# A two-layer encoder trunk on one core: GpSimd's copies and adding transfers form four input blocks of the MLP's up product

## The chip, the cores and the metric

The kernel runs on one core of a Trainium2 chip. Its engines are TensorE (PE, matrix products into the PSUM banks), VectorE (DVE), ScalarE (ACT), GpSimd (POOL) and SyncE (SP); the last two mostly start transfers here, which run on the core's 16 DMA engines. Each engine works through its own queue in order, and the queues wait for each other by semaphores alone. The metric is the device time of one execution in microseconds, as the median of runs; less is better.

## The reference

```python
def sqrelu_mlp(h, w_up, w_down):
    a = jax.nn.relu(h @ w_up)
    return (a * a) @ w_down

def reference(x, norm_mix, conv_w_in, conv_w, conv_w_out, attn_w_qkv, attn_rpb,
              attn_w_o, norm_mlp, mlp_w_up, mlp_w_down, norm_final):
    for i in range(DEPTH):
        h = rmsnorm(x, norm_mix[i])
        ...
            x = x + short_conv_mixer(h, conv_w_in[j], conv_w[j], conv_w_out[j])
        ...
            x = x + neighborhood_attention_2d(h, attn_w_qkv[j], attn_rpb[j], attn_w_o[j])
        h = rmsnorm(x, norm_mlp[i])
        x = x + sqrelu_mlp(h, mlp_w_up[i], mlp_w_down[i])
    return rmsnorm(x, norm_final)
```

DEPTH is 2, the sequence has 512 tokens of 1024 features, the MLP is 4096 wide, and everything is float32.

## The kernel before

**Every float32 product is three products.** An operand is split into a rounding (w_h, a_h, hx), made by ScalarE, and a rest (w_l, a_l, and the second half of hx), made by VectorE as operand minus rounding; TensorE multiplies rounding by rounding, rounding by rest and rest by rounding (L588 to L590). The weights come in 282 units w of 128x1024. For each unit ScalarE does hi(w) (L908), which waits for the unit's data and for TensorE to have finished unit w-4; VectorE does lo(w) (L1178), which waits for hi(w); TensorE waits for the lo of the unit that it starts. w_h and w_l have four slots each.

**Big products are done in seven instead of eight block products.** The matrices of the MLP are cut in quarters Y11, Y12, Y21, Y22 of 128x2048 (1 MB each, two units each), and seven products P1 to P7 take sums of them: T1 = Y12 - Y11, written over Y12, goes into P5, T2 = T1 - Y22 into P6, T3 = Y11 + T2 into P7 and T4 = Y21 + T2 into P4. T1 and T2 are VectorE's (sums_of_y, L1222 and L1228). T3 and T4 are adding transfers that GpSimd starts (add_sums(q), L528 and L530, for matrix q): T3 when T2 is made and the units of P1 are split, T4 when those of P2 are. A block product with the down matrix is called product 0 to 6 of second(tc) and has two units; the order is P1, P2, P6, P5, P7, P3, P4 (NORMAL) at the places that matter here.

**The two MLPs** (n = 0 and 1) each multiply the first 1024 of the 4096 features in the plain way (eight units), then run second(1 + 4n) with the down matrix, then for c = 1 to 3 up_seven(n, c) and second. second(1) is units 46 to 59, matrix 1; up_seven(0, 1) is units 60 to 73, matrix 2. Matrix q + 1 is loaded by SP in the order Y12, Y11, Y22, Y21 into rooms that come free: its Y12 when x_sums of the first MLP chunk is done, its Y11 only when T3 and T4 of matrix q have landed, since it goes to T2's room.

**The input blocks.** up_seven takes seven blocks of the MLP's input a_h + a_l: P1 to P4 are quarters of it, P5, P7, P6 and the new P3 are sums. They are formed once per MLP, in the two buffers sum_raw[0] and sum_raw[1] (t0 and t1): VectorE puts P3, P4, P1 and P2 together from rounding and rest (in_raw, L1232), adds and subtracts (in_sums(n, i), L1242 to L1255), ScalarE rounds a sum (in_round, L970), and VectorE makes its rest (in_rest, L1259). Semaphores: in_sum counts sums, in_hi roundings, in_lo rests. up_seven(n, 1) is the first to read them.

**What sets the order** is the text of each engine's program alone. In the loop over the eight plain units (m = 0 to 7) VectorE has in_sums(0) at m = 3, in_sums(1) and (2) at m = 4 and 5, in_rest(0) and (1) at m = 6 and 7, and in_sums(3), the block of P1, behind the loop, ahead of lo(49). Within second(1), lo(first + 2 pos + 3) starts product pos, evict(pos) (L1338) takes the finished product out of PSUM, and lo(first + 2 pos + 4) ends it; T1 of the next matrix stands behind evict(3).

Of the kernel before, what the change touches and what calls it, by code (L numbers as in the profile page):

```python
# [4 lines left out]
P = 128  # L5
D = 1024
SEQ = 512
KT = D // P
HEADS = 16
HD = D // HEADS  # L10
ROWS, GW, WIN = 8, 64, 16
CHUNKS = 4
# [176 lines left out]
def encoder(nc, x, x_tok, wave, weights, blocks, small, gains, rpb, out):  # L189
# [3 lines left out]
    with ctx:  # L193
# [192 lines left out]

        in_sum = sem("in_sum")
# [134 lines left out]
        def _(pool):  # L522
# [8 lines left out]

            def load_bias(j):
                if j > 1:
                    pool.wait_ge(s_free, 2 * (j - 1))
                pool.dma_start(head_bias[j % 2], bias_dram[:, 2 * j:2 * j + 2, :]).then_inc(bias_in[j % 2], 16)

# [28 lines left out]
            for q in range(SEQ_ATTN):  # L565
                add_sums(q)

            pool.wait_ge(w_split, second_first(CHUNKS) + 14)
            pool.memset(v_shift[3][HD:P, :], 0.0).then_inc(shift_zero, 1)
            for half in range(2):  # L570
                pool.wait_ge(v_got, 4 * (half + 1))
                f = slice(512 * half, 512 * half + 512)
                for s in range(4):
                    if s:
                        pool.dma_start(v_shift[s - 1][HD:P, f], v_tile[s][0:HD, f]).then_inc(v_in, 16)
                    pool.dma_start(v_shift[s][0:HD, f], v_tile[s][HD:P, f]).then_inc(v_in, 16)
            pool.wait_ge(tiles_in, 16 * 3 * WIN)
            pool.wait_ge(tr_done, 16)
            for j in range(KT):
                load_bias(j)  # L580
            for q in range(SEQ_ATTN, N_MATRIX):
                add_sums(q)
# [317 lines left out]
        def _(act):  # L900
# [77 lines left out]
            def up_seven(n, c):  # L978
                tb, tc = 3 * n + c - 1, 1 + CHUNKS * n + c
                first = MATRIX[7 * n + 2 * c][0]  # L980
                for pos in range(7):
# [11 lines left out]
                    elif pos == 2:  # L993
                        nc.scalar.activation(X_BLOCK["X21"], up_pair("P6"), ACT.Copy).then_inc(up_copy, 1)
                        if c == 1:
                            in_round(n, 3)
                    elif pos == 3:
                        nc.scalar.activation(X_BLOCK["X11"], up_pair("P5"), ACT.Copy).then_inc(up_copy, 1)
# [57 lines left out]
            def mlp(n):  # L1056
                tc = 1 + CHUNKS * n
                for m in range(KT):
# [9 lines left out]
                    if m in (5, 6):  # L1068
                        in_round(n, m - 5)
# [93 lines left out]
        def _(dve):  # L1163
# [561 lines left out]
```

## Time and profile before

| | us |
|---|---|
| median of 3 runs (1068.30 to 1068.61) | 1068.36 |
| the profiled execution | 1068.09 |
| its span in the trace | 1066.3 |
| PE busy | 1050.7 (99%) |
| DVE busy | 801.7 (75%) |
| ACT busy | 558.9 (52%) |
| POOL busy | 82.1 (8%) |

The profile is of one execution. The span is what the trace covers; the rest of the execution's time, 1.8 us, lies around it. Busy is the time in which an engine has an instruction in work; transfers don't count as busy time of the engine that starts them. Names in rows are those of the program without buffer numbers, so every room of weights and both sum_raw buffers are called big; L588 is line 588.

### The profile page before, as it was taken

Reading aid. Unit: us, or ns where it says so; the run is one execution under the profiler, and the core shown is the slowest. Engines: PE = TensorE matmul, PEld = TensorE weight load, DVE = VectorE, ACT = ScalarE, POOL = GpSimd, SP = SyncE. Lnnn points to the kernel's source line nnn. Section 1 sums busy time; section 2 is a strip of 40 time slices with the busy share of each in tenths; the row PEclk is TensorE's granted clock in tenths of the full one; section 3 lists DMA queues with packets and bytes.
Section 4 is the critical chain, followed back from the end, with each engine's and each line's share of the span. In section 5 each row is a group of like instructions: output and inputs, shape, how many; then the busy total and the mean of one; then the engine's idle time right before and its main releaser. Section 6 shows DMA issues by size and latency. Waiting matters only on the chain.

```text
span 1066.3 us, 15177 instructions
## 1 busy us (share of the span) xinstructions
PE 1050.7 (99%) x6088; PEld 910.8 (85%) x6088; DVE 801.7 (75%) x1124; ACT 558.9 (52%) x781; POOL 82.1 (8%) x132
## 2 busy tenths in 40 slices
PE   9999999999999999999999999999999999999996
PEld 7888888977998988988877777779977988988984
DVE  5886688699798598598426666636799798697696
ACT  6131256564674574576424443426663674674663
POOL 2353000000000000000110000000000000000000
PEclk9999999999999999999999999999999999999998
DMA  7994264035746646642454323252055547457332
GB/s 241 374 367 144 79 158 138 21 78 199 198 119 178 178 119 188 168 119 64 139 162 132 108 86 106 60 237 80 1 119 185 171 128 207 146 137 202 129 74 84
DMA packets 32245, 155.30 MB, mean 146 GB/s; under 512 B 5232, under 2 KB 5360, under 8 KB 20656
## 3 DMA queue, kind: packets, MB, share of 16 engines
q1 hardware_dynamic: 21600, 102.80, 27.4%
q0 software_dynamic: 10576, 51.54, 20.6%
q8 instruction: 48, 0.79, 0.3%
q14 instruction: 21, 0.17, 0.0%
HBM read 113.80 MB, written 10.48 MB: 117 GB/s over the span
## 4 chain that ended last, share of the span: by engine, by line
PE 96%; DVE 2%; ACT 1%; issue 1%; DMA 0%; DVEq 0%; SPq 0%; ACTq 0%
PE bank L588 30%; PE bank L590 30%; PE bank L589 30%; PE bank L786 2%; PE bank L768 1%; PE bank L753 1%; PE bank L611 1%; DVE w_l L1178 0%; DVE xs L1323 0%; ACT big L936 0%; DMA big<-x 0%; DVE big L1232 0%; DVE sx L1259 0%; DVE hx L1183 0%; ACT w_h L908 0%
## 5 line engine op out<-in xcount | busy, mean ns | idle before, releaser
L908 ACT ACTIVATE w_h<-big 128x1024 fp32r<-128x1024 f32 x210 | 221.7, 1058 | 224.5 <-PE bank L590 224.4
L588 PE MATMUL bank<-a_h,w_h 128*128 128x256 f32 (+1 forms) x896 | 296.7, 331 | 0.4 <-DVE w_l L1502 0.4
L590 PE MATMUL bank<-a_h,w_l 128*128 128x256 f32 (+1 forms) x896 | 294.5, 329 | 0.0
L589 PE MATMUL bank<-a_l,w_h 128*128 128x256 f32 (+1 forms) x896 | 294.4, 329 | 0.0
L1178 DVE TENSOR_TENSOR w_l<-big,w_h 128x1024 fp32r<-128x1024 f32 x210 | 250.7, 1221 | 23.0 <-ACT w_h L908 22.8
L588 PE MATMUL bank<-w_h,hx 128*128 128x512 f32 x568 | 222.9, 392 | 2.3 <-DVE w_l L1178 2.3
L590 PE MATMUL bank<-w_h,hx 128*128 128x512 f32 x568 | 221.1, 389 | 0.0
L589 PE MATMUL bank<-w_l,hx 128*128 128x512 f32 x568 | 221.1, 389 | 0.0
L588 PEld LDWEIGHTS bank<-a_h,w_h 128*128 128x128 f32 x896 | 170.3, 190 | 18.2 <-issue 3.6
L590 PEld LDWEIGHTS bank<-a_h,w_l 128*128 128x128 f32 x896 | 170.3, 190 | 15.3
L589 PEld LDWEIGHTS bank<-a_l,w_h 128*128 128x128 f32 x896 | 170.4, 190 | 14.8 <-issue 0.2
L908 ACT ACTIVATE w_h<-raw 128x1024 fp32r<-128x1024 f32 x67 | 70.5, 1059 | 134.9 <-PE bank L590 103.1
L588 PEld LDWEIGHTS bank<-w_h,hx 128*128 128x128 f32 x568 | 106.6, 188 | 28.2 <-issue 5.5
L590 PEld LDWEIGHTS bank<-w_h,hx 128*128 128x128 f32 x568 | 106.6, 188 | 22.5
L589 PEld LDWEIGHTS bank<-w_l,hx 128*128 128x128 f32 x568 | 106.7, 188 | 21.3
L1178 DVE TENSOR_TENSOR w_l<-raw,w_h 128x1024 fp32r<-128x1024 f32 x67 | 81.6, 1219 | 27.4 <-ACT w_h L908 27.0
L588 PE MATMUL bank<-sx,w_h 128*128 128x256 f32 x288 | 81.5, 283 | 0.0
L589 PE MATMUL bank<-sx,w_h 128*128 128x256 f32 x288 | 81.5, 283 | 0.0
L590 PE MATMUL bank<-sx,w_l 128*128 128x256 f32 x288 | 81.5, 283 | 0.0
L528 POOL DMA_DIRECT2D big<-big x15 | 13.1, 876 | 595.4 <-DVE w_l L1178 595.4
L588 PEld LDWEIGHTS bank<-sx,w_h 128*128 128x128 f32 x288 | 55.3, 192 | 0.0
L589 PEld LDWEIGHTS bank<-sx,w_h 128*128 128x128 f32 x288 | 55.3, 192 | 0.0
(142 smaller groups left out, 1177.0 us busy)
## 6 DMA issues: line engine op xcount, KB each, us to landing
big<-blocks SPq DMA_DIRECT2D x56, 1024.0 KB, 5.0
raw<-weights SPq DMA_DIRECT2D x68, 512.0 KB, 3.7
big<-big POOLq DMA_DIRECT2D x30, 1024.0 KB, 7.2
bias_tiles<-big POOLq DMA_DIRECT2D x8, 624.0 KB, 11.0
big<-bias_tiles POOLq DMA_DIRECT2D x8, 624.0 KB, 4.1
big<-blocks POOLq DMA_DIRECT2D x4, 1024.0 KB, 27.2
bias_tiles<-bias_rows POOLq DMA_DIRECT2D x48, 64.0 KB, 11.5
big<-x SPq DMA_DIRECT2D x8, 256.0 KB, 5.4
```

Source lines behind the costliest of these rows:

```text
L528: pool.dma_start(room[at["Y11"]], room[at["T2"]], accum_op=ALU.add).then_inc(t3_in, 16)
L588: nc.tensor.matmul(dst, sh, mh, start=start, stop=False, skip_group_check=again)
L589: nc.tensor.matmul(dst, sh, ml, start=False, stop=False, skip_group_check=again)
L590: return nc.tensor.matmul(dst, sl, mh, start=False, stop=stop, skip_group_check=again)
L611: last = nc.tensor.transpose(bank[b][:, at:at + P], xn[2 * half + t][:, P * k:P * k + P], ident[:])
L753: last = nc.tensor.matmul(score[par_][:, score_at(half, n)], qT[rows, P * b:P * b + P], kT[rows, ROWS * c0:ROWS * (c0 + nk)], start=True, ...
L768: last = nc.tensor.transpose(tposed[par_][0:width, P * t:P * t + P], prob[half][:, at + P * c:at + P * c + width], ident[:])
L786: last = nc.tensor.matmul(attn_out[rows, P * b:P * b + P], V_AT[b][c][keys, feats], probT[half][keys, at:at + P], start=c == 0, stop=c == 1)
L908: nc.scalar.activation(wh_all[:, w % SLOTS, :], src, ACT.Copy).then_inc(w_hi, 1)
L1178: nc.vector.tensor_tensor(wl_all[:, s, :], src, wh_all[:, s, :].bitcast(f32), ALU.subtract).then_inc(w_split, 1)
```

## The change

The eight instructions of VectorE that put P3, P4, P1 and P2 together (in_raw, four in each MLP) are replaced by transfers that GpSimd starts: raw_copy copies the rounding a_h into sum_raw[i], and raw_add adds the rest a_l to it, when the copy has landed (in_copy). in_raw now is a semaphore that counts those sums, and VectorE waits for it. The copies of P3 and P4 wait for the MLP's normed input (a_ready), that of P1 for the second rest (in_lo), since it overwrites sum_raw[0], that of P2 for the third sum (in_sum). On GpSimd all this stands ahead of add_sums(7n + 1), but for P2's pair, which stands behind it.

On VectorE in_sums(1) and (2) move from m = 4 and 5 to m = 5 and 6, in_rest(0) and (1) from m = 6 and 7 to behind the loop, in_sums(4) from product 1 to product 3 of second, in_rest(2) from product 4 of second to product 0 of up_seven, in_sums(6) there from 1 to 2, in_rest(3) from 3 to 4; ScalarE's in_round moves with them. T1 of the next matrix moves from product 3 to product 4 in the second() of both MLPs' first chunks (tc = 1 and 5).

```diff
+            def raw_copy(i, name):
+
+                pool.dma_start(sum_raw[i], u_part(name, False).bitcast(f32)).then_inc(in_copy, 16)
+
+            def raw_add(n, i, name, count):
+
+                pool.wait_ge(in_copy, 16 * (4 * n + count))
+                pool.dma_start(sum_raw[i], u_part(name, True).bitcast(f32), accum_op=ALU.add).then_inc(in_raw, 16)
+
+            def input_blocks(n):
+                pool.wait_ge(a_ready, a_place(2 * n + 1, 1) + KT)
+                raw_copy(0, "P3")
+                raw_copy(1, "P4")
+                raw_add(n, 0, "P3", 2)
+                raw_add(n, 1, "P4", 2)
+                pool.wait_ge(in_lo, 4 * n + 2)
+                raw_copy(0, "P1")
+                raw_add(n, 0, "P1", 3)
+
+            def input_block_late(n):
+                pool.wait_ge(in_sum, 4 * n + 3)
+                raw_copy(0, "P2")
+                raw_add(n, 0, "P2", 4)
...
-            for q in range(SEQ_ATTN):
-                add_sums(q)
...
+            add_sums(0)
+            for n in range(2):
+                input_blocks(n)
+                add_sums(7 * n + 1)
+                input_block_late(n)
+                for q in range(7 * n + 2, 7 * n + 8):
+                    add_sums(q)
+                if n == 0:
+                    attention()
...
-                        if tc and pos == 2:
+                        if tc and pos == 4:
                             in_round((tc - 1) // CHUNKS, 2)
...
-                    if m in (5, 6):
-                        in_round(n, m - 5)
+                    if m in (6, 7):
+                        in_round(n, m - 6)
...
-            def in_raw(i, name):
-
-                link(nc.vector.tensor_tensor(sum_raw[i], u_part(name, False).bitcast(f32), u_part(name, True).bitcast(f32),
-                                             ALU.add))
...
-                if i == 0:
-                    in_raw(0, "P3")
-                    in_raw(1, "P4")
-                elif i == 1:
+                if i == 1:
+                    dve.wait_ge(in_raw, 16 * (4 * n + 2))
                     nc.vector.tensor_tensor(t1, t0, t1, ALU.add).then_inc(in_sum, 1)
...
-                elif i == 3:
-                    dve.wait_ge(in_lo, 4 * n + 2)
-                    in_raw(0, "P1")
                 elif i == 4:
+                    dve.wait_ge(in_raw, 16 * (4 * n + 3))
                     nc.vector.tensor_tensor(t1, t0, t1, ALU.subtract).then_inc(in_sum, 1)
-                elif i == 5:
-                    dve.wait_ge(in_sum, 4 * n + 3)
-                    in_raw(0, "P2")
-                else:
+                elif i == 6:
+                    dve.wait_ge(in_raw, 16 * (4 * n + 4))
                     nc.vector.tensor_tensor(t0, t0, t1, ALU.add).then_inc(in_sum, 1)
...
-                    if pos == 3 and n is None:
+                    if pos == (4 if tc in BY_UNIT else 3) and n is None:
                         sums_of_y(seq_of(tc) + 1, 0)
...
-                    if m > 2:
-                        in_sums(n, m - 3) if m < 6 else in_rest(n, m - 6)
-                in_sums(n, 3)
+                    if m in (5, 6):
+                        in_sums(n, m - 4)
+                in_rest(n, 0)
+                in_rest(n, 1)
                 second(tc)
```

**GpSimd's queue behind the tiles of the attention bias, before.** T3 and T4 of matrix 0, then of matrix 1:

```order
L564 DMA bias_tiles<-bias_rows 128x1x128 x47
L528 DMA big<-big 128x2048 [waits w_split,t_sum]
L530 DMA big<-big 128x2048 [waits w_split]
L528 DMA big<-big 128x2048 [waits w_split,t_sum]
L530 DMA big<-big 128x2048 [waits w_split]
```

**The same place now** (L530 and L532 are T3 and T4, L536 and L541 the copies and adding transfers of the input blocks):

```order
L530 DMA big<-big 128x2048 [waits w_split,t_sum]
L532 DMA big<-big 128x2048 [waits w_split]
L536 DMA big<-a_h 128x4x256 [waits a_ready]
L536 DMA big<-a_h 128x4x256
L541 DMA big<-a_l 128x4x256 [waits in_copy] x2
L536 DMA big<-a_h 128x4x256 [waits in_lo]
L541 DMA big<-a_l 128x4x256 [waits in_copy]
L530 DMA big<-big 128x2048 [waits w_split,t_sum]
L532 DMA big<-big 128x2048 [waits w_split]
L536 DMA big<-a_h 128x4x256 [waits in_sum]
L541 DMA big<-a_l 128x4x256 [waits in_copy]
```

Between T4 of matrix 0 and T3 of matrix 1 now stand the pairs of P3, P4 and P1, behind a wait for a_ready and one for in_lo; the pair of P2 stands behind T4 of matrix 1.

**VectorE at the end of the loop over the plain units, before.** L1183 are rests of the MLP's hidden blocks, L1259 is in_rest(1), L1232 the block of P1, and L1178 lo(49):

```order
L1183 TENSOR_TENSOR hx<-big,hx 128x256 [waits x_hi] x2
L1259 TENSOR_TENSOR sx<-big,sx 128x1024 [waits in_hi]
L1232 TENSOR_TENSOR big<-a_h,a_l 128x1024 [waits in_lo]
L1178 TENSOR_TENSOR w_l<-big,w_h 128x1024 [waits w_hi,chain]
L1183 TENSOR_TENSOR hx<-big,hx 128x256 [waits x_hi] x2
```

**The same place now** (L1217, L1283, L1212 for these lines; L1364 is evict(0)):

```order
L1217 TENSOR_TENSOR hx<-big,hx 128x256 [waits x_hi] x2
L1283 TENSOR_TENSOR sx<-big,sx 128x1024 [waits in_hi] x2
L1212 TENSOR_TENSOR w_l<-big,w_h 128x1024 [waits w_hi]
L1217 TENSOR_TENSOR hx<-big,hx 128x256 [waits x_hi] x2
L1364 TENSOR_TENSOR xs<-bank,xs 128x2x512 [waits adds,unit_done]
```

Both rests now stand behind the loop, and P1's block is gone.

**VectorE from evict(2) of second(1) on, before** (L1338 evict, L1178 lo, L1222 T1 of matrix 2, L1259 in_rest(2)):

```order
L1338 TENSOR_TENSOR xs<-bank,xs 128x2x512 [waits adds,unit_done]
L1178 TENSOR_TENSOR w_l<-big,w_h 128x1024 [waits w_hi]
L1183 TENSOR_TENSOR hx<-big,hx 128x1024 [waits x_hi]
L1178 TENSOR_TENSOR w_l<-big,w_h 128x1024 [waits w_hi]
L1338 TENSOR_TENSOR xs<-bank,xs 128x2x512 [waits adds,unit_done]
L1222 TENSOR_TENSOR big<-big 128x2048 [waits Y11_in,Y12_in]
L1178 TENSOR_TENSOR w_l<-big,w_h 128x1024 [waits w_hi]
L1183 TENSOR_TENSOR hx<-big,hx 128x1024 [waits x_hi]
L1178 TENSOR_TENSOR w_l<-big,w_h 128x1024 [waits w_hi]
L1259 TENSOR_TENSOR sx<-big,sx 128x1024 [waits in_hi]
```

**The same place now** (L1364 evict, L1212 lo, L1276 in_sums(4), L1256 T1):

```order
L1364 TENSOR_TENSOR xs<-bank,xs 128x2x512 [waits adds,unit_done]
L1212 TENSOR_TENSOR w_l<-big,w_h 128x1024 [waits w_hi]
L1217 TENSOR_TENSOR hx<-big,hx 128x1024 [waits x_hi]
L1212 TENSOR_TENSOR w_l<-big,w_h 128x1024 [waits w_hi]
L1276 TENSOR_TENSOR big<-big 128x1024 [waits in_raw]
L1364 TENSOR_TENSOR xs<-bank,xs 128x2x512 [waits adds,unit_done]
L1212 TENSOR_TENSOR w_l<-big,w_h 128x1024 [waits w_hi]
L1217 TENSOR_TENSOR hx<-big,hx 128x1024 [waits x_hi]
L1212 TENSOR_TENSOR w_l<-big,w_h 128x1024 [waits w_hi]
L1364 TENSOR_TENSOR xs<-bank,xs 128x2x512 [waits adds,unit_done]
L1256 TENSOR_TENSOR big<-big 128x2048 [waits Y11_in,Y12_in]
L1212 TENSOR_TENSOR w_l<-big,w_h 128x1024 [waits w_hi] x2
```

in_sums(4) came in ahead of evict(3), and T1 moved from behind evict(3), ahead of lo(56), to behind evict(4), ahead of lo(58).

## Rows read from the trace of the kernel before

**Rows 1.** Part 1 of the page: busy time (share of the span) xinstructions.
```profile
PE 1050.7 (99%) x6088; PEld 910.8 (85%) x6088; DVE 801.7 (75%) x1124; ACT 558.9 (52%) x781; POOL 82.1 (8%) x132
```

**Rows 2.** Waits of TensorE, whole kernel: total, times, longest.
```profile
PE bank L588 <- DVE w_l L1178: 2.3, 4, 1.2
```

**Rows 3.** Timeline of TensorE: start, us, instruction [idle before, releaser].
```profile
233.91 0.50 PE L588 MATMUL bank<-w_h,hx 128*128 128x512 f32 x1 [0.24 <-DVE w_l L1178]
...
254.17 0.47 PE L588 MATMUL bank<-w_h,hx 128*128 128x512 f32 x1 [0.62 <-DVE w_l L1178]
...
265.44 0.36 PE L588 MATMUL bank<-a_h,w_h 128*128 128x256 f32 x1
...
808.95 0.47 PE L588 MATMUL bank<-w_h,hx 128*128 128x512 f32 x1 [1.23 <-DVE w_l L1178]
...
820.22 0.36 PE L588 MATMUL bank<-a_h,w_h 128*128 128x256 f32 x1
```

**Rows 4.** Timeline of VectorE, the first MLP, last row the second.
```profile
230.12 1.22 DVE L1259 TENSOR_TENSOR sx<-big,sx 128x1024 fp32r<-128x1024 f32 x1
231.37 1.22 DVE L1232 TENSOR_TENSOR big<-a_h,a_l 128x1024 f32<-128x1024 f32 x1
232.63 1.22 DVE L1178 TENSOR_TENSOR w_l<-big,w_h 128x1024 fp32r<-128x1024 f32 x1
...
250.59 2.29 DVE L1222 TENSOR_TENSOR big<-big 128x2048 f32<-128x2048 f32 x1 [1.17 <-DMA big<-blocks]
252.80 1.22 DVE L1178 TENSOR_TENSOR w_l<-big,w_h 128x1024 fp32r<-128x1024 f32 x1
253.94 1.22 DVE L1183 TENSOR_TENSOR hx<-big,hx 128x1024 fp32r<-128x1024 f32 x1
...
294.50 1.23 DVE L1266 TENSOR_TENSOR big<-bank,big 128x1024 f32<-128x1024 f32 x1 [2.63 <-PE bank L590]
...
786.80 1.22 DVE L1178 TENSOR_TENSOR w_l<-big,w_h 128x1024 fp32r<-128x1024 f32 x1
```

**Rows 5.** Timeline of GpSimd: T3 and T4 of matrix 1.
```profile
222.14 0.86 POOL L528 DMA_DIRECT2D big<-big  x1 [76.60 <-DVE w_l L1178]
234.15 0.86 POOL L530 DMA_DIRECT2D big<-big  x1 [11.15 <-DVE w_l L1178]
```

**Rows 6.** Transfers: the view of DMA issues, then lines L528, L530, L499.
```profile
big<-blocks SPq DMA_DIRECT2D x56, 1024.0 KB, 5.0
...
big<-bias_tiles POOLq DMA_DIRECT2D x8, 624.0 KB, 4.1
...
big<-big POOLq DMA_DIRECT2D x14, 128.0 KB, 2.6
...
L528 POOL DMA_DIRECT2D big<-big x15: 861/870/979, 136.0 to 1017.1; - x15
...
DMA to landing us min/median/max: 6.9/7.0/9.2
...
L530 POOL DMA_DIRECT2D big<-big x1: 861/861/861, 234.1 to 234.1; - x1
...
DMA to landing us min/median/max: 11.4/11.4/11.4
...
L499 SPq DMA_DIRECT2D big<-blocks x1: 328/328/328, 234.6 to 234.6; - x1
...
DMA to landing us min/median/max: 8.2/8.2/8.2
```

**Rows 7.** Timelines of ScalarE (three rows) and VectorE (one).
```profile
240.04 1.06 ACT L908 ACTIVATE w_h<-big 128x1024 fp32r<-128x1024 f32 x1 [0.99 <-PE bank L590]
242.76 1.06 ACT L908 ACTIVATE w_h<-big 128x1024 fp32r<-128x1024 f32 x1 [1.66 <-PE bank L590]
...
271.52 1.06 ACT L908 ACTIVATE w_h<-big 128x1024 fp32r<-128x1024 f32 x1 [1.82 <-PE bank L590]
...
272.62 1.23 DVE L1178 TENSOR_TENSOR w_l<-big,w_h 128x1024 fp32r<-128x1024 f32 x1 [0.39 <-ACT w_h L908]
```

More of the change, by code:

```diff
@@ L385, in encoder @@
         adds = sem("adds")
+        in_copy = sem("in_copy")
+        in_raw = sem("in_raw")
         in_sum = sem("in_sum")
@@ L535, in load_bias, with attention @@
                 pool.dma_start(head_bias[j % 2], bias_dram[:, 2 * j:2 * j + 2, :]).then_inc(bias_in[j % 2], 16)
+            def attention():
+                pool.wait_ge(w_split, second_first(CHUNKS) + 14)
+                pool.memset(v_shift[3][HD:P, :], 0.0).then_inc(shift_zero, 1)
+                for half in range(2):
+                    pool.wait_ge(v_got, 4 * (half + 1))
+                    f = slice(512 * half, 512 * half + 512)
+                    for s in range(4):
+                        if s:
+                            pool.dma_start(v_shift[s - 1][HD:P, f], v_tile[s][0:HD, f]).then_inc(v_in, 16)
+                        pool.dma_start(v_shift[s][0:HD, f], v_tile[s][HD:P, f]).then_inc(v_in, 16)
+                pool.wait_ge(tiles_in, 16 * 3 * WIN)
+                pool.wait_ge(tr_done, 16)
+                for j in range(KT):
+                    load_bias(j)
             pool.memset(ones[:], 1.0).then_inc(const_ready, 1)
@@ L564, in _ @@
                     pool.dma_start(dst, src).then_inc(tiles_in, 16)
-            for q in range(SEQ_ATTN):
-                add_sums(q)
[L568 to L582, printed above, removed]
+            add_sums(0)
[7 more added lines that the diff above has]
+                    attention()
         @block.tensor
@@ L994, in up_seven @@
                         nc.scalar.activation(X_BLOCK["X21"], up_pair("P6"), ACT.Copy).then_inc(up_copy, 1)
+                    elif pos == 3:
+                        nc.scalar.activation(X_BLOCK["X11"], up_pair("P5"), ACT.Copy).then_inc(up_copy, 1)
                         if c == 1:
                             in_round(n, 3)
-                    elif pos == 3:
-                        nc.scalar.activation(X_BLOCK["X11"], up_pair("P5"), ACT.Copy).then_inc(up_copy, 1)
                     elif pos == 4:
@@ L1295, in up_seven @@
                     lo(first + 2 * pos + 3)
-                    if c == 1 and pos in (0, 1):
-                        in_sums(n, 5 + pos)
-                    if c == 1 and pos == 3:
+                    if c == 1 and pos == 0:
+                        in_rest(n, 2)
+                    if c == 1 and pos == 2:
+                        in_sums(n, 6)
+                    if c == 1 and pos == 4:
                         in_rest(n, 3)
@@ L1397, in second @@
                             x_sums(tc, 3)
-                        if tc and pos == 1:
+                        if tc and pos == 3:
                             in_sums((tc - 1) // CHUNKS, 4)
-                        if tc and pos == 4:
-                            in_rest((tc - 1) // CHUNKS, 2)
                     elif pos == 0:
```

1 line of the change is left out of this document (added).

## The prediction

> **What bounds the kernel now.** I read the busy shares first: TensorE is busy for 1050.7 of 1066.3 us [rows 1], so a change can only move time where TensorE runs dry, or make it run dry in new places. Then the waits of TensorE: 2.3 us on the rests w_l of VectorE [rows 2]. Then the timeline at those places. In the first MLP the product with chunk 0 of the down matrix (second(1), units 46 to 59) stands still before units 49 and 56, for 0.24 and 0.62 us, and in the second MLP the second such stop is 1.23 us [rows 3]. From the start of unit 49 at 233.91 to that of unit 60 at 265.44 lie eleven units of 2.72 us (hi(54) and hi(55), each started when TensorE let it, at 240.04 and 242.76 [rows 7]), 29.9 us, where the trace has 31.5; with the first stop that is 1.9 us lost, and 2.5 us in the second MLP, whose unit 60 comes 0.6 us later on the same scale (below). These 4.4 us are all that the change can win. The cause of the longest one is visible on VectorE: T1 of the next matrix waits 1.17 us for a load, begins at 250.59, takes 2.21 us, and only then comes the rest of unit 56 at 252.80 [rows 4].
>
> The sum is made on the profiled execution, 1068.09 us with a span of 1066.3; the median of the three runs is 1068.36, so I add differences to the median.
>
> **What the change takes away.** VectorE loses eight instructions of 128x1024 (four blocks in each MLP). A block costs 1.24 us there, 231.37 to 232.63 [rows 4], so 10 us of VectorE in all; but only those just ahead of a stop count. The two in the loop over the up units and the one in the next up product lie where TensorE never waits (rows 2 list all its waits for VectorE's w_l, four in the kernel): worth nothing. The one at 231.37 is replaced by the second in_rest, moved to the same place, which costs 1.13 instead of 1.24 us and starts 0.1 us sooner by lack of a link behind it: lo(49) goes from 232.63 to about 232.4, and the first stop shrinks from 0.24 to about 0, unit 50 follows; 0.25 us per MLP. T1 at product 4 instead of product 3 no longer stands ahead of lo(56), which takes away the stop at 254.17 and its refill (0.7 us; 1.3 us in the second MLP), if VectorE arrives there on time.
>
> **What the change adds, and whose way it is in.** GpSimd's queue is strictly in order. Ahead of add_sums(1), whose first transfer is T3 (Y11 += T2, 1 MB, for product P7), now stands the copy of P1, which waits for in_lo, that is for the second in_rest of VectorE, and the adding transfer of P1, which waits for the copy. Before, T3 was issued at 222.14 and T4 at 234.15 [rows 5]; unit 54, the first of P7, was rounded by ScalarE (hi(54)) at 240.04, when TensorE let it, so T3 (7.0 us, [rows 6]) had 240.0 − 229.1 = 11 us to spare [rows 7]. Worked anew, with the second in_rest in the place of the block at 231.37:
> - the second in_rest starts at 230.12 + 1.13 = 231.25 and ends 1.22 us later, 232.5. GpSimd answers 0.3 us later (lo(49) ended at 232.63 + 1.22 = 233.85, T4 was issued at 234.15): the copy of P1 is issued at 232.8.
> - the trace has no copy of 512 KB within SBUF. The nearest rows: 128 KB within SBUF 2.6 us, 624 KB from HBM 4.1 us [rows 6]. These two are the bounds; on the line between them 512 KB take 3.8 us, and I take 3.7, a little to the side of the one within SBUF: landed at 236.5.
> - 0.3 us later, 236.8, the add of P1 is issued. T3 stands right behind it in the same queue. What grows with the size is 7.0 − 2.6 = 4.4 us from 128 KB to the 1 MB of T3 [rows 6], so 2.5 us for the 512 KB of P1 that are ahead of T3 in the queue. T3 lands at 236.8 + 2.5 + 7.0 = 246.3 on an otherwise quiet set of DMA engines.
> - they aren't quiet: SP's first load of the next matrix goes out at 234.3 (before: 234.6). Beside that load T4 took 11.4 instead of 7.0 us, and the load 8.2 instead of its median 5.0 [rows 6]. So this costs between 0 and 4.4 us. At its median the load would be over at 239.3, and half of it before P1's add is issued, where T4 had the whole of it beside it; I take a quarter of the 4.4, 1.1, nearer to the quiet end for that reason: T3 lands at L = **247.4**. Both ends together: 245.2 (copy 2.6, load 0) to 251.1 (copy 4.1, load 4.4, the rest as before).
>
> The Trainium skill speaks against this size: "DMA: Bandwidth & Descriptors" (Anatomy of one DMA) gives a transfer on GpSimd's path 2.0 us plus its bytes at 436 GB/s. By that T3 alone would take 4.4 us, where the trace has 7.0 [rows 6]; the page times plain transfers, and these read and write the target. What this would do here is the second rival.
>
> **From L to TensorE.** ScalarE's hi(54) starts at L + 0.1. ScalarE to VectorE takes 1.1 us (hi at 271.52, lo at 272.62 [rows 7]), so lo(54) = L + 1.2 = 248.6. TensorE takes a unit 1.37 us after its lo starts (252.80 to 254.17, [rows 3, 4]) and a unit every 2.72 us (hi 240.04 to 242.76, [rows 7]), so, three units after the end of unit 50 that let hi(54) go at 240.04, it wants unit 54 at about 247.7 (the 0.25 us won taken off) and gets it at 250.0: a new stop of 2.3 us. Behind lo(54) VectorE has no gap left: up to lo(60) come twelve instructions at 1.135 us (252.80 to 253.94, [rows 4]), 13.6 us, among them the in_sums moved to product 3, and two T sums at 2.21 us, 4.4 us. So lo(60) = L + 1.2 + 18.0, and unit 60 starts at L + 1.2 + 18.0 + 1.4 = **L + 20.6** = 268.0. On the way unit 58 waits too: its rest now stands behind T1 at product 4, lo(58) = L + 1.2 + 12.4 = 261.0, TensorE is ready for it at 261.0 and gets it at 262.4, 1.4 us more. T1's load doesn't add to this: it goes out when T4 has landed (5.0 us behind T3, by the 2.5 us for 512 KB) and lands 5.0 us later, L + 10.0, ahead of VectorE at L + 11.4. The other waits have cover: P2's copy and add are released at about 253 and wanted behind lo(65), which stood at 272.62 before [rows 7], twice the longest transfer; and the last rest, moved one product on, falls into a pause of 2.63 us that VectorE had there [rows 4]. If that cover were gone it would cost one instruction, 1.1 us.
>
> Before, unit 60 started at 265.44 in the first MLP; in the second, where the same instructions stand 554.17 us later (lo(49) at 786.80), at 820.22, that is 266.05 on the first one's scale [rows 3, 4]. The change costs (L + 20.6 − 265.4) + (L + 20.6 − 266.05) = **2L − 490.3** us, since TensorE, with no slack ahead, never gives a delay back. For L = 247.4 that is +4.5 us: 1068.36 + 4.5 = 1072.9.
>
> **The rivals.**
> - *T3 lands late, but just late enough to eat the gain.* L = 245.2 gives +0.1 us, 1068.5; within 0.2% (2.1 us, about what a measurement here can tell from no change) up to L = 246.2. For it: the add of P1 is only half a transfer and the load may be over. Against it: load and copy share the same engines from 235 on. 0.14.
> - *The other side: T3 is in time.* It needs L below 244.1 to show as faster; with lo(54) started by 245.0 the product keeps only the small stops at units 49 and 50 (0.5 us) and TensorE reaches unit 60 at 264.1: −1.3 − 1.9 = −3.3 us, 1065.1. It would happen if transfers out of SBUF cost far less than rows 6 say: with a copy of 2.6 us and the queue moving P1's half in 1.2 instead of 2.5 us, L = 243.9. Against it: every T3 of the trace took 6.9 us or more [rows 6]. 0.10. (By the Trainium skill's page "DMA: Bandwidth & Descriptors", Anatomy of one DMA, with 3.2 us for the copy and 2.0 us plus 1.5 MB at its rate behind it, an estimate is L of about 242, which is this rival.)
> - *The load blocks the queue as it did T4.* T4's delay of 4.4 us on top of the quiet 246.3 gives L = 250.7, +11 us, 1079.5; from L = 249.5 on (over 1077) I count it here. 0.10.
> - *The change doesn't do what it says*, the copy of P1 not holding back T3: excluded by the order of one queue.
>
> **How the numbers follow.** Forecast (L from 246.2 to 249.5) 0.66, rivals 0.14, 0.10, 0.10. Slower 0.76, same 0.14, faster 0.10. The range takes in the forecast and the first rival, 1068.2 to 1077, and leaves out the other two.
>
> **What would show it.** In the trace of the changed kernel: T3 of matrix 1 issued near 237.7 instead of 222.1, landing near 247; hi(54) waiting for a DMA; a stop of TensorE of about 2 us before unit 54 (near 250) and one of about 1.4 us before unit 58 (near 262), the same 554 us later plus the delay; unit 60 near 268.0. The stop at 254 gone. I am wrong if hi(54) still starts at 240 with TensorE as its releaser, or if VectorE catches up before lo(58).

## The result, and the profile after

| | before | after |
|---|---|---|
| median, us | 1068.61 (1068.30 to 1069.49) | 1073.90 (1073.27 to 1074.31) |
| the profiled execution, us | 1068.09 | 1074.14 |
| its span, us | 1066.3 | 1072.3 |
| mean granted clock of TensorE | 0.997 | 0.993 |

The ratio is 1.0049, with a 95% interval of 1.0038 to 1.0061: slower, by 5.3 us (half a per cent). The forecast was +4.5 us, to 1072.9, and the range 1068.2 to 1077 holds the time.

The busy shares of the page after, the waits of TensorE for VectorE's w_l, and a wait of ScalarE that was not there before (total, times, longest):

```profile
PE 1054.0 (98%) x6088; PEld 913.8 (85%) x6088; DVE 792.0 (74%) x1116; ACT 558.2 (52%) x781; POOL 98.1 (9%) x148
...
PE bank L622 <- DVE w_l L1212: 5.4, 3, 2.4
...
ACT w_h L942 <- DMA big<-big: 17.8, 2, 9.0
```

VectorE has lost the 10 us that the edit takes off it (792.0 where it had 801.7 [rows 1]), and TensorE waits 5.4 us for its rests where it waited 2.3 [rows 2]. The last line says why: twice, once in each MLP, ScalarE's rounding of a unit waits 9 us for a transfer between rooms, which is T3.

The timeline of GpSimd in the first MLP shows the new queue (start, us, instruction, [idle before, releaser]): the copy of P1, its add, T3, T4. Before, T3 stood at 222.14 and T4 at 234.15 [rows 5].

```profile
233.96 0.78 POOL L536 DMA_DIRECT2D big<-a_h  x1 [31.61 <-DVE sx L1283]
238.15 1.27 POOL L541 DMA_DIRECT2D big<-a_l  x1 [3.40 <-DVE w_l L1212]
238.90 1.41 POOL L530 DMA_DIRECT2D big<-big  x1
239.46 1.75 POOL L532 DMA_DIRECT2D big<-big  x1
```

T3's time from issue to landing, in the view of line L530, first MLP, then second:

```profile
DMA to landing us min/median/max: 9.8/9.8/9.8
...
DMA to landing us min/median/max: 10.3/10.3/10.3
```

T3 lands at 238.9 + 9.8 = 248.7. Behind it come ScalarE's hi(54), VectorE's lo(54), T1, lo(58) and lo(60), and TensorE's units 54 and 60 of the first MLP, then those of the second (the timelines of the three engines):

```profile
248.74 2.00 ACT L942 ACTIVATE w_h<-big 128x1024 fp32r<-128x1024 f32 x2 [8.76 <-DMA big<-big]
```

```profile
249.82 1.23 DVE L1212 TENSOR_TENSOR w_l<-big,w_h 128x1024 fp32r<-128x1024 f32 x1 [4.90 <-ACT w_h L942]
...
260.04 2.28 DVE L1256 TENSOR_TENSOR big<-big 128x2048 f32<-128x2048 f32 x1
262.24 2.36 DVE L1212 TENSOR_TENSOR w_l<-big,w_h 128x1024 fp32r<-128x1024 f32 x2
...
267.85 2.35 DVE L1212 TENSOR_TENSOR w_l<-big,w_h 128x1024 fp32r<-128x1024 f32 x2
```

```profile
251.20 0.47 PE L622 MATMUL bank<-w_h,hx 128*128 128x512 f32 x1 [2.15 <-DVE w_l L1212]
...
269.25 0.32 PE L622 MATMUL bank<-a_h,w_h 128*128 128x256 f32 x1
...
808.23 0.47 PE L622 MATMUL bank<-w_h,hx 128*128 128x512 f32 x1 [2.43 <-DVE w_l L1212]
...
826.27 0.33 PE L622 MATMUL bank<-a_h,w_h 128*128 128x256 f32 x1
```

Against rows 3, unit 60 comes 3.8 us later in the first MLP (269.25 against 265.44), and in the second 6.05 us (826.27 against 820.22). Of the 3.8, 1.1 us is older: in this execution TensorE waited for the load of a weight unit at 57 us, ahead of all changed code (unit at 58.33 where the execution of before had it at 57.24). So the first MLP costs 2.7 us and the second 2.25.

One thing was not forecast. Two stretches of the profile: from and to, length, busy time (and count) of PE, PEld, DVE, ACT and POOL, then the granted clock, the DMA share and GB/s:

```profile
251.20:252.40 1.20, 1.20 (x5) 1.01 (x6) 1.20 (x2) 1.20 (x2) 0.00 (x0) 1.00 1.04 212
252.40:255.80 3.40, 3.40 (x9) 2.63 (x8) 3.40 (x4) 1.28 (x3) 0.79 (x1) 0.50 0.41 101
```

1.2 us after TensorE has taken up unit 54, its clock falls to half (1.2 GHz) for 3.4 us, and matmuls start 0.43 instead of 0.23 us apart. From 255.8 on it is full again. The same happens in the second MLP. After the stop of 1.23 us at 808.95 in the kernel before [rows 3] the clock had stayed full.

### The profile page after: what moved, and what is told of

It reads as the page before. It is cut to its first block, busy times and chain, and to the rows that moved or that the text cites. A ratio compares the mean times of both kernels' runs of the same rounds, so it can differ in the third digit from the quotient of the medians.

```text
span 1072.3 us, 15181 instructions
## 1 busy us (share of the span) xinstructions
PE 1054.0 (98%) x6088; PEld 913.8 (85%) x6088; DVE 792.0 (74%) x1116; ACT 558.2 (52%) x781; POOL 98.1 (9%) x148
## 4 chain that ended last, share of the span: by engine, by line
PE 90%; DMA 4%; DVE 2%; issue 1%; ACT 1%; SPq 1%; POOL 0%; DVEq 0%; POOLq 0%; ACTq 0%
PE bank L622 28%; PE bank L624 28%; PE bank L623 28%; DMA big<-big 2%; DMA raw<-weights 2%; PE bank L820 2%; PE bank L802 1%; PE bank L787 1%; PE bank L645 1%; SPq L483 1%; ACT w_h L942 0%; PE bank L835 0%; DVE w_l L1212 0%; DVE sx L1283 0%; DVE xs L1349 0%
## 5 line engine op out<-in xcount | busy, mean ns | idle before, releaser
L1212 DVE TENSOR_TENSOR w_l<-big,w_h 128x1024 fp32r<-128x1024 f32 x210 | 250.4, 1219 | 34.5 <-ACT w_h L942 31.5
L1212 DVE TENSOR_TENSOR w_l<-raw,w_h 128x1024 fp32r<-128x1024 f32 x67 | 81.6, 1219 | 33.9 <-ACT w_h L942 29.1
L624 PEld LDWEIGHTS bank<-sx,w_l 128*128 128x128 f32 x288 | 55.3, 192 | 0.0
```

Source lines behind the costliest of these rows:

```text
L624: return nc.tensor.matmul(dst, sl, mh, start=False, stop=stop, skip_group_check=again)
L1212: nc.vector.tensor_tensor(wl_all[:, s, :], src, wh_all[:, s, :].bitcast(f32), ALU.subtract).then_inc(w_split, 1)
```

## The experiments

Diffs are against the changed kernel unless another is named. The theory: the loss is T3 behind P1's pair in one queue, one us per us of T3 in each MLP, and the moved T1 is a gain of its own. The rivals: T1's new place or the wait for in_lo does harm; the load from SyncE, not the queue, delays T3; the fallen clock carries the loss.

### The T1 move alone

```diff
-                    if pos == 3 and n is None:
+                    if pos == (4 if tc in BY_UNIT else 3) and n is None:
```

This edit is on the kernel before.

> The kernel before with one edit: T1 of the next matrix behind product 4 instead of 3 in the first chunks; VectorE still forms all blocks. In the trace of the changed kernel the stops at units 56, 58 and 60 were gone by 1.1 us in the first MLP and 1.7 us in the second, and I put that down to this edit alone: 1068.5 - 2.8 = 1065.7. The rival that the relief comes from the instructions taken from VectorE expects no gain, 1068.5.

Measured: 1065.53 us against 1068.99 of before, ratio 0.9968 [0.9956, 0.9981]. Of TensorE's waits for w_l this is left, in an execution that again had the 1 us at 57:

```profile
PE bank L588 <- DVE w_l L1178: 1.5, 3, 1.0
```

The move is a gain of 3.5 us (3.0 in the traces, from the start of unit 54 to that of unit 60 in both MLPs) where 2.0 (0.7 + 1.3) were forecast for it. The expectation's own figure, 2.8, was too small as well. So the changed kernel loses not 5.3 us by its other parts but nearly 9.

### The wait alone

The kernel of the last experiment with the wait for the second in_rest ahead of add_sums(1) and (8):

```diff
             for q in range(SEQ_ATTN):
+                if q == 1:
+                    pool.wait_ge(in_lo, 2)
                 add_sums(q)
...
```

> As e2_t1_only, and GpSimd waits for the second rest (in_lo) ahead of T3 and T4 of the MLP's first matrix, but has no copies and adds. T3 is then issued near 231.7 instead of 222.1, and should land near 240 to 242, where hi(54) has some 2.8 us of room: the same as e2_t1_only, 1065.7, at most 1 us more. If the wait alone, and not the transfers behind it, were the cause, it would cost some 4 us, about 1070.

Measured: 1066.36 us, ratio 0.9971 [0.9960, 0.9983]. T3 is issued at 232.0 where the trace of the last experiment has 223.8 (and everything in this MLP 1.2 us later), and nothing waits for it. The wait costs nothing that can be told apart; the transfers behind it do the harm.

### T3 ahead of the pair

add_sums(q) is split into add_t3(q) and add_t4(q); add_t4 stays where add_sums(7n + 1) was, and in input_blocks(n):

```diff
                 raw_add(n, 1, "P4", 2)
+                add_t3(7 * n + 1)
                 pool.wait_ge(in_lo, 4 * n + 2)
                 raw_copy(0, "P1")
```

> The changed kernel with T3 of the MLP's first matrix started ahead of the wait for in_lo and of P1's copy and add; T4 stays behind them. My theory (the late T3 holds hi(54) and VectorE's whole chain behind it) expects T3 issued at about 222 us again, no stop of TensorE before unit 54, TensorE's clock full throughout, T4 landing by 248 and T1 at product 4 without a wait: about 3.3 us less than before, 1065.2 (1064.5 to 1066.5). The rival that the added transfers as such, or the new places of VectorE's sums, cost the time expects it to stay near the changed kernel's 1073.9.

Measured: 1065.12 us, ratio 0.9963 [0.9951, 0.9976]. The whole loss is gone with one transfer in another place. The timeline of GpSimd (T3, copy, add; T4 follows at 238.07) and hi(54) on ScalarE, released by TensorE's bank as in rows 7:

```profile
223.93 0.87 POOL L530 DMA_DIRECT2D big<-big  x1 [22.41 <-DVE w_l L1221]
233.18 0.78 POOL L544 DMA_DIRECT2D big<-a_h  x1 [8.38 <-DVE sx L1292]
237.31 1.27 POOL L549 DMA_DIRECT2D big<-a_l  x1 [3.35 <-DMA big<-a_h]
...
240.17 1.06 ACT L951 ACTIVATE w_h<-big 128x1024 fp32r<-128x1024 f32 x1 [0.97 <-PE bank L633]
```

All waits of TensorE on this kernel's list:

```profile
PE bank L844 <- POOL ident L592: 1.7, 1, 1.7
PE bank L796 <- DVE big L1654: 0.8, 1, 0.8
PE bank L631 <- DVE w_l L1536: 0.2, 1, 0.2
```

It beats the kernel before by 3.9 us. But the T1 move alone gave 3.5 of them, and the intervals overlap: that VectorE is spared 10 us of additions is worth 0.4 us or nothing.

### P1's pair halved

Copy and add of P1 take only half of the block, so half of P1 is left out of the sum:

```diff
+                ks = slice(0, 2) if name == "P1" else slice(0, 4)
-                pool.dma_start(sum_raw[i], u_part(name, True).bitcast(f32), accum_op=ALU.add)...
+                pool.dma_start(sum_raw[i][:, ks, :], u_part(name, True)[:, ks, :].bitcast(f32), accum_op=ALU.add)...
```

(the copy in the same way)

> The changed kernel with P1's copy and add cut to the first two of four slices (256 KB each); the other half of P1's part of one sum is left out. T3 should land about 2.7 us earlier than in the changed kernel (1 us from the copy, 1.3 to 2 from the add). By my sum the time goes with twice that landing: 1073.9 - 5.4 = 1068.5 (1067 to 1070); TensorE's stop before unit 54 nearly gone, its clock full, and a stop of about 1.2 us before unit 58 in its place. If the fallen clock behind the stop of 2.1 us were what costs, the gain would be the clock's 1.7 us per MLP plus the stop and no stop would show before unit 58.

Measured: 1070.42 us, ratio 1.0012 [1.0003, 1.0021], 3.5 us less than the changed kernel where 5.4 were expected. T3's time from issue to landing, and the two stops of TensorE in the first MLP, before units 54 and 58:

```profile
DMA to landing us min/median/max: 9.3/9.3/9.3
...
249.30 0.47 PE L624 MATMUL bank<-w_h,hx 128*128 128x512 f32 x1 [0.33 <-DVE w_l L1214]
...
261.71 0.47 PE L624 MATMUL bank<-w_h,hx 128*128 128x512 f32 x1 [1.01 <-DVE w_l L1214]
```

T3 lands at 237.5 + 9.3 = 246.8, 1.9 us sooner (1.5 in the second MLP), where 2.7 were expected. The time followed: unit 60 comes 1.9 us sooner in the first MLP and 1.4 more in the second. What was wrong is how much the half pair brings. It reaches the queue while SyncE's load is still at work: the add is issued at 236.75, and its first packet moves at 239.5, with the load's last ones; that is 2.7 us behind the issue, where it is 1.8 in the changed kernel. With the full clock (0.996) that this execution kept, the stop before unit 58 is there, 1.01 us, that the forecast had put at 1.4 and that was missing in the changed kernel.

### The load out of the way

SyncE's first load of the next matrix waits for T3:

```diff
                 for role in LOAD_ORDER:
...
+                    if role == LOAD_ORDER[0] and q in (2, SEQ_ATTN + 1):
+                        sp.wait_ge(t3_in, 16 * q)
```

> The changed kernel with one wait more on SyncE: the first load of the next matrix (Y12) goes out in both MLPs only when T3 has landed, so it no longer shares the DMA engines with P1's pair and T3. This measures the load's part in T3's delay. In the changed kernel T3 lands 10.6 us after the add of P1 is issued (238.15 to 248.7). By the forecast's terms (2.5 us for P1's half, 7.0 for T3, 1.1 for the load) it now lands 9.5 us behind it, the stop before unit 54 shrinks from 2.15 to about 1.05 us, and each us of T3 is a us of the kernel in each MLP: 1073.9 - 2.2 = 1071.7. The rival, for which the run with P1's pair halved speaks (T3 landed 10.0 us behind the add there, though the pair had 1.25 us less to move): the load costs 2 to 3 us and the pair ahead in the queue less than 2.5; then T3 lands 7.6 to 8.6 us behind the add and the time is 1068.5 to 1070. In both the granted clock should stay full, as the stop is short. T1 needs the late load only at about 258, it lands near 252.

Measured: 1076.20 us, ratio 1.0071 [1.0051, 1.0091]: both theories missed. The times to landing of T3 and of T4, and T1 on VectorE:

```profile
DMA to landing us min/median/max: 9.8/9.8/9.8
...
DMA to landing us min/median/max: 15.6/15.6/15.6
...
261.56 2.29 DVE L1258 TENSOR_TENSOR big<-big 128x2048 f32<-128x2048 f32 x1 [1.44 <-DMA big<-blocks]
```

T3 takes 9.8 us from its issue with the load beside the pair and 9.8 without, in the first MLP. What the load costs there is 0.3 us, and ahead of the add: from the copy's issue to the add's it is 3.9 us here and 4.2 in the changed kernel. In the second MLP it is 0.3 for the copy and 0.4 for T3 (9.9 against 10.3). TensorE's stops before unit 54 shrink by as much, from 2.15 to 1.89 and from 2.43 to 1.72 us. So the forecast's term of 1.1 us behind the add is nothing in the first MLP and 0.4 in the second. T3 still landed at the right time, so another term was as much too small. The packets of GpSimd's queue (q0) in the changed kernel show which. First the stretch of P1's add, 239.5 to 243.1, then that of T3, 243.2 to 248.5 (packets, MB, share of the 16 engines):

```profile
q0 software_dynamic: 507, 0.54, 103.6%
```

```profile
q0 software_dynamic: 164, 1.12, 104.6%
```

P1's 512 KB move as 512 packets of 1 KB in 3.3 us, from 239.9 on; T3's 1 MB as 128 packets of 8 KB, landed 5.0 us behind P1's sum. SyncE's load had moved its last 8 KB packets at 239.8, just as the add's first ones came, 1.8 us behind the add's issue; with the load held back they came 1.8 us behind it too. The forecast had 2.5 us for P1. The median is 2.3 us above the changed kernel's, with four runs from 1074.06 to 1080.16: the load is now beside T4, which lands at 255.1 instead of 253.7; the load of Y11, which waits for T4, comes later, and T1 waits 1.44 us for it, 0.28 in the second MLP. The two profiled executions are 1.2 us apart.

### P1 copied twice

```diff
                 raw_copy(0, "P1")
-                raw_add(n, 0, "P1", 3)
+                pool.wait_ge(in_copy, 16 * (5 * n + 3))
+                raw_copy(0, "P1")
+                raw_add(n, 0, "P1", 4)
```

> The changed kernel with the copy of P1 made twice, one after the other, ahead of its add: T3 is issued 4.2 us later (a copy takes 4.0 us from issue to landing and 0.2 us goes to the next issue). This measures the slope of the time on T3's landing, and lengthens the stop before unit 54. If the chain of VectorE behind lo(54) has no gap and the load is still as much in the way as it was, the time is 1073.9 + 2 x 4.2 = 1082.3. If the load's 1.1 us goes away, as it is over before the add is issued, T3 lands 3.1 us later: 1080.1. If part of the delay can be made up (VectorE has gaps up to lo(60)), it is below 1079. The granted clock should be 0.5 again for some 3 to 4 us behind the stop of 5 to 6 us before unit 54; if the clock's fall adds to the time by itself, and isn't only hidden where TensorE would have waited for VectorE anyway, it comes out above 1083.

Measured: 1085.19 us, ratio 1.0150 [1.0136, 1.0164], in the place named for a clock whose fall costs by itself. By the trace that is the smaller part, about half a us. The timeline of GpSimd in the first MLP, T3's landing, and unit 54:

```profile
234.61 0.78 POOL L536 DMA_DIRECT2D big<-a_h  x1 [31.61 <-DVE sx L1285]
238.68 0.77 POOL L536 DMA_DIRECT2D big<-a_h  x1 [3.29 <-DMA big<-a_h]
242.83 1.32 POOL L541 DMA_DIRECT2D big<-a_l  x1 [3.38 <-DMA big<-a_h]
243.60 1.47 POOL L530 DMA_DIRECT2D big<-big  x1
...
DMA to landing us min/median/max: 9.8/9.8/9.8
...
255.93 0.76 PE L624 MATMUL bank<-w_h,hx 128*128 128x512 f32 x1 [6.26 <-DVE w_l L1214]
```

T3 lands at 253.4, 10.6 us behind the add's issue as there, though no load is near. That is 4.7 us later than in the changed kernel, of which 0.6 are the wait at 57 us, longer in this execution (its unit starts at 58.97 instead of 58.33); 4.1 are due to the copy. In the second MLP the second copy took 6.6 us from its issue to the add's, beside a load, and T3 landed 6.0 us later than in the changed kernel, measured from the start of the fourth unit of that MLP's second(5). 4.1 + 6.0 = 10.1; the two profiled executions are 11.2 us apart, 10.6 without the wait at 57, and the medians 11.3. The slope of one to one carries nearly all of it, and what was wrong is the price of the second copy.

The clock fell for 6.8 and 10.2 us, and here it costs something of its own. Unit 60 of the first MLP on TensorE:

```profile
274.29 0.28 PE L624 MATMUL bank<-a_h,w_h 128*128 128x256 f32 x1
```

Its rest starts at 272.61, so VectorE allows it at 274.0, 1.4 us later. TensorE comes 0.3 us behind that: it has lost more time at half clock than VectorE's instructions would have made it wait. In the second MLP unit 60 is 6.3 us later where T3 is 6.0. Together that is about the half us between 10.1 and 10.6.

### T1 back at product 3

The kernel with T3 ahead of the pair, and:

```diff
-                    if pos == (4 if tc in BY_UNIT else 3) and n is None:
+                    if pos == 3 and n is None:
```

> The kernel with T3 ahead of P1's pair (1065.1), with T1 of the next matrix put back from product 4 to product 3: of the gain that kernel shows, is T1's place the whole? And it makes a stop of about 3 us before unit 56 by another way than T3. T1 needs the load of Y11, which goes out when T4 has landed, at 247.84 in that kernel, and lands about 4.95 us later (245.65 to 250.59 before the change): T1 starts at 252.8, lo(56) at 255.0, unit 56 at 256.4 where TensorE wants it at 253.3. A stop of 3.1 us in each MLP, 3.7 in the second: 1065.1 + 6.8 = 1071.9 with a full clock. If a stop of that length halves the granted clock as the one of 2.15 us in the changed kernel did, TensorE loses 1.65 us more in each MLP, and VectorE, which isn't behind it here, can't hide it: 1075.2. If T1's place has nothing to do with the gain: 1065.

Measured: 1073.88 us (1071.31 to 1076.16), ratio 1.0043 [1.0030, 1.0056], between the two values. T1 on VectorE, unit 56 on TensorE in the first MLP, and the stretch of half clock in the second:

```profile
252.76 2.29 DVE L1265 TENSOR_TENSOR big<-big 128x2048 f32<-128x2048 f32 x1 [3.02 <-DMA big<-blocks]
...
256.34 0.47 PE L631 MATMUL bank<-w_h,hx 128*128 128x512 f32 x1 [2.71 <-DVE w_l L1221]
...
811.90:818.70 6.80, 6.13 (x15) 4.81 (x16) 6.80 (x7) 0.57 (x1) 1.27 (x1) 0.50 0.75 218
```

In the first MLP T1 comes at 252.76 (expected 252.8) and unit 56 at 256.34 (256.4). So the pair needs the T1 move: T4, behind it, lands 2.2 us later than before the change, and with it the load that T1 reads. The clock of this execution stayed full after the stop of 2.71 us in the first MLP and fell in the second, after one of 3.3. Here VectorE isn't behind, and the clock shows in the time: from the start of unit 56 to that of unit 60 TensorE takes 10.97 us in the first MLP (256.34 to 267.31) and 13.89 in the second (812.57 to 826.46), 2.9 us more. Of the six executions, those with a mean clock of 0.997 took 1071.31, 1072.49 and 1073.55 us, and those with 0.991 to 0.994 took 1074.21 to 1076.16.

### T3 between copy and add

```diff
                 raw_copy(0, "P1")
+                add_t3(7 * n + 1)
                 raw_add(n, 0, "P1", 3)
```

> The changed kernel with T3 of matrix 1 (and 8) issued between P1's copy and P1's add, in the time in which GpSimd would only wait for the copy. T3 is issued at about 235 instead of 238.9. Beside the copy and the load it takes 7.0 to 11.4 us and lands at 242 to 246.4, ahead of TensorE's wish for unit 54 (247.7): no stop there, P1's add behind it is wanted only at 251. The time is that of the kernel with T3 ahead of the whole pair, 1065.1 (1064.5 to 1065.8). The rival: P1's add, queued behind T3, and T4 behind that become late, T4's landing (before: 245.6, here about 249) holds back the load of Y11 and so T1 at product 4, or in_sums waits for P1: then 1066 to 1068, with TensorE waiting before unit 58 or 56.

Measured: 1075.02 us, ratio 1.0057 [1.0044, 1.0069]. The rival's mechanism, at a price far above the 1 to 3 us given for it. T1 on VectorE, and unit 58, in the first MLP:

```profile
259.31 2.29 DVE L1265 TENSOR_TENSOR big<-big 128x2048 f32<-128x2048 f32 x1 [2.80 <-DMA big<-blocks]
...
262.88 0.77 PE L631 MATMUL bank<-w_h,hx 128*128 128x512 f32 x1 [3.72 <-DVE w_l L1221]
```

T3, issued at 233.97 beside the load, takes 11.1 us and still lands in time for TensorE (245.1); in the second MLP it takes 12.7, and TensorE waits 0.87 us before unit 54. But the add waits behind it, T4 behind the add, and T4 lands at 252.7. The load of Y11 goes out then, beside P2's copy and add, and takes 6.6 us instead of 5.0; T1 waits 2.80 us and TensorE 3.72. I had counted T4 at 249. The clock adds to the price: after the stop of 3.72 us it is half for 6.8 us, and unit 60 starts 8.1 us behind unit 58, where the second MLP, with a stop of 2.93 us and a full clock, has 5.6.

### Both T3 and T4 ahead

```diff
                 raw_add(n, 1, "P4", 2)
+                add_sums(7 * n + 1)
                 pool.wait_ge(in_lo, 4 * n + 2)
```

> The changed kernel with T3 and T4 of matrix 1 (and 8) both ahead of P1's pair: in the queue's order of before the change, the pair behind. T4 goes out at 234.15, beside the load at 234.6, and lands at 245.6 as before the change. If the queue moves its bytes strictly in order, as the records of the run with T3 between copy and add suggest, the copy of P1 (issued 235) moves only behind T4: landed 247.4, its add issued 247.6, first packet 1.8 us later, 3.3 us of packets, landed 252.9. VectorE's in_sums(4), which stood at 247.4 in the kernel with T3 first, waits until 253.1, then come a bank and lo(56) at 255.4, unit 56 at 256.8 where TensorE wants it at 253.3: 3.5 us in each MLP, 1065.1 + 7.0 = 1072.1, and up to 1077 where the granted clock falls after such a stop. If the copy's packets go between those of T4, P1 lands by 245, nothing waits, and the time is 1065.

Measured: 1088.97 us, ratio 1.0186 [1.0172, 1.0200], 12 us above the most that was expected. The copy and the add of P1 on GpSimd, the add's landing, and in_sums(4) on VectorE:

```profile
235.09 1.10 POOL L536 DMA_DIRECT2D big<-a_h  x1
247.85 1.29 POOL L541 DMA_DIRECT2D big<-a_l  x1 [11.66 <-DMA big<-a_h]
...
DMA to landing us min/median/max: 11.4/11.4/11.4
...
259.32 1.23 DVE L1276 TENSOR_TENSOR big<-big 128x1024 f32<-128x1024 f32 x1 [11.57 <-DMA big<-a_l]
```

The copy of P1 lands at 247.3, expected 247.4: in the queue it moves only when T4 has. The add was to land at 252.9 and lands at 259.2, 11.4 us after its issue. T4's landing at 245.9 lets go three loads, with packets of 8 KB, and the add is slow beside them in two ways. The queues of SyncE (q1) and GpSimd (q0), first from 248.0 to 252.5, then from 252.5 to 256.5:

```profile
q1 hardware_dynamic: 228, 1.74, 96.5%
q0 software_dynamic: 1, 0.00, 0.1%
...
q1 hardware_dynamic: 154, 1.12, 78.9%
q0 software_dynamic: 123, 0.13, 19.4%
```

The add's packets begin only at 252.4, 4.5 us behind its issue, where the changed kernel has 1.8; why they wait, no run shows. From then on the two queues get nearly the same share packet for packet, 154 and 123, but in bytes GpSimd's gets a ninth. That two queues take turns on each engine by packets is what the Trainium skill states in "DMA: Bandwidth & Descriptors" (Queues, rings and completion order); the counts of the second stretch agree with it, those of the first do not.

### P1's add with long rows

```diff
-                pool.dma_start(sum_raw[i], u_part(name, True).bitcast(f32), accum_op=ALU.add).then_inc(in_raw, 16)
+                if name == "P1":
+                    pool.dma_start(big[:, 16384:17408], big[:, 17408:18432], accum_op=ALU.add).then_inc(in_raw, 16)
...
```

> The changed kernel with P1's add reading the other sum buffer instead of the rest a_l, so that source and target both have rows of 4 KB in each partition (it adds other values: the rest of P1 is left out of the sum). The same 512 KB. In the changed kernel this add moves in 512 packets of 1 KB in 3.3 us. If that is due to the short rows, it now moves at T3's rate (1 MB in 5.3 us), in 2.6 us, T3 lands 0.6 us sooner (10.0 us behind the add's issue instead of 10.6), and the time is 1.2 us less, 1072.7, or 1069.5 to 1071 if the shorter stop lets the granted clock stay full. If an adding transfer of 512 KB takes its 3.3 us in any form: 1073.9.

Measured: 1073.58 us (1071.75 to 1074.71), ratio 1.0043 [1.0030, 1.0057]: by time, not to be told from the changed kernel. The trace is clear. GpSimd's queue in the stretch of the add (some 120 packets of 4 KB), T3's landing, and unit 54:

```profile
q0 software_dynamic: 129, 0.53, 101.7%
...
DMA to landing us min/median/max: 9.4/9.4/9.4
...
249.20 0.47 PE L625 MATMUL bank<-w_h,hx 128*128 128x512 f32 x1 [1.32 <-DVE w_l L1215]
```

The add moves in 2.6 us, T3 lands 10.0 us behind the add's issue instead of 10.6, and the profiled execution, 1071.75, is 1.3 us under that of the changed kernel once the 1.1 us at 57 is taken off. So some 0.6 to 0.7 of the 3.3 us are due to rows of 1 KB. The Trainium skill, "DMA: Bandwidth & Descriptors" (Why small descriptors are slow (HBM only)), says that transfers within SBUF don't suffer from small descriptors; for an adding transfer, 3.3 against 2.6 us for the same bytes, this case differs from it.

## Why the prediction was right

**The bound and the gain.** Right in kind. The first stop went (unit 49 came 0.2 us sooner, forecast 0.25) and the stop before unit 56 too, but the T1 move alone is worth 3.5 us where the steps had 2.0, and the kernel with T3 in time reached 1065.12 where the rival had 1065.1 (3.9 us under the runs of before that were made with it, where the rival had 3.3).

**T3's landing, L.** Forecast 247.4; read 248.7 less the 1.1 us from 57 on, 247.6. The terms one by one, on the scale of before:

| term | forecast | trace |
|---|---|---|
| copy of P1 issued | 232.8 | 232.9 |
| copy, issue to landing | 3.7 | 3.6 |
| from there to the add's issue | 0.3 | 0.6 |
| add issued | 236.8 | 237.1 |
| P1's half in the queue | 2.5 | 3.6 (3.3 us of packets, 0.3 more) |
| the load of the next matrix | 1.1 | 0.0 |
| T3 by itself (median of rows 6, taken for both) | 7.0 | 7.0 |

Two steps failed and cancelled each other, so that L came out within 0.2 us is luck. The load's 1.1 us was interpolated between an overlap that the trace before had (T4, issued 0.4 us ahead of the load) and none; the packets show the load over when the add's began, and the run with the load held back gave the same 9.8 us. That holds for this timing: with the pair halved the add was issued sooner, with the load still at work, and its first packet came 0.9 us later behind its issue than here. P1's half was sized by bytes on a line between 128 KB and 1 MB, and it took 1.1 us more; its short rows, which bytes don't tell, are 0.6 to 0.7 of that, by the run with long rows.

One reading of the rows was off without harm: T3 had not 11 but 9.8 us to spare, since in that place it took 8.1 us before the change (222.14 to 230.2) and not the median of 7.0.

**From L to unit 60.** The rule L + 20.6 held to 0.1 us wherever T3 was last and VectorE set the pace (first MLP):

| kernel | T3 lands | + 20.6 | unit 60 starts |
|---|---|---|---|
| changed | 248.7 | 269.3 | 269.25 |
| pair halved | 246.8 | 267.4 | 267.3 |
| add with long rows | 246.7 | 267.3 | 267.2 |
| copied twice | 253.4 | 274.0 | 274.3 (TensorE late by its clock) |

From lo(54) to lo(60) it is 18.03 us in the changed kernel, as forecast (18.0): VectorE has no gap. It fails where T1's load comes last, with T3 in between (unit 60 at 271.0 where L + 20.6 is 265.7; 2.5 us of that is the clock). The steps had said that T1's load is there at L + 10.0, 1.4 us ahead of VectorE; they didn't say how near that margin is to nothing once something is put between T3 and T4.

**The two stops.** Before unit 54 2.3 us were forecast, and it is 2.15. Before unit 58 1.4 us were forecast and there is none: TensorE, at half clock for 3.4 us, came to unit 58 only when its rest was there. With a full clock the stop is there (1.01 us with the pair halved). The end is the same, but only just: unit 60 starts at 269.25, and its rest, begun at 267.85, allowed it 1.4 us later, at 269.2. TensorE had just made up for the fall; with a longer one, in the kernel that copies twice, it had not. The one execution of the changed kernel that had a mean clock of 0.996 took 1073.84 us, those with 0.993 from 1073.27 to 1074.31.

**The rest.** 2.7 + 2.25 us in the two MLPs, where the forecast had 2.6 + 1.95; the medians differ by 5.3. The remaining 0.3 us is not traced to a place. The edits costed at nothing cost nothing: with T3 in time TensorE's list of waits has only 0.2 us for w_l, though P2's copy takes 11.0 us in the changed kernel beside three loads, some three times the 3.4 to 4.3 of those of P1, P3 and P4. Its cover held: its add went out at 266.06 and landed 7.9 us later, at 274.0, and VectorE took the sum only at 284.4.

## What to carry to other kernels

A transfer that replaces an engine's work stands in the order of a queue: ask what is urgent behind it there, put that ahead, and then ask the same of the one behind that. Size a transfer by its packets as well as its bytes: the adding transfer with short rows was slower alone (3.3 against 2.6 us), and lost far more to long-rowed loads beside it (11.4 us). An offload from an engine that isn't the bound gains only what it takes from the instructions just ahead of a stop; here one instruction moved by one product in each MLP gave nearly all of it.

## What the runs showed of the hardware

- The granted clock fell to half after stops of 1.89 us (the first MLP of the run with the load held back), 2.12 (the add with long rows, second MLP), 2.15 and 2.43 us (changed kernel), 3.3 us and more, and stayed full after stops of 1.23 us (before), 1.72 (the load held back, second MLP), 2.71 us (T1 back at product 3, first MLP) and 2.93 us (T3 between copy and add, second MLP). Between 1.9 and 2.9 us the length of a stop alone doesn't decide it. The falls lasted 3.4, 6.8 or 10.2 us; those of 6.8 and 10.2 began within the stop, those of 3.4 behind it. What else decides was not tried.
- What a fall costs depends on who is behind: nothing that can be seen in the changed kernel, where VectorE sets the pace; 0.3 us in the first MLP of the kernel that copies twice, where TensorE fell just behind it; 2.5 us (T3 between copy and add) and 2.9 us (T1 back at product 3) where VectorE doesn't set it.
- GpSimd's transfers to one queue moved one after the other, also when they were issued 0.6 us apart: T4, issued at 239.46, moved only from 248.6 on.
- P1's copy of 512 KB within SBUF took 3.6 us from issue to landing in the changed kernel, and its adding transfer, of the same size from rows of 1 KB, 5.6 us with nothing ahead of it (up to 8.0 for the eight of the kernel, 11.4 beside three loads); one of 1 MB with rows of 8 KB took 6.9 us or more.
